# Products of constants that nobody reads, put on TensorE's queue in five places of a two-block transformer kernel

## The chip, the cores and the metric

The kernel runs on one core of one Trainium2 chip. The metric is the device time of one execution in microseconds. The names of the engines in the rows: PE is TensorE (matmul), PEld its weight load, DVE is VectorE, ACT is ScalarE, POOL is GpSimd, SP is SyncE.

## The reference: what is computed

Two blocks follow each other on a sequence of 512 tokens of width 1024 (8 tiles of 128 features), all in float32.

```
# first block: condition, normalise, project, two mixers, project out
mod = silu(c) @ w_ada + b_ada;  shift, scale, gate = split(mod, 3)
h = rms_norm(x, norm_g) * (1 + scale) + shift
ssm_u, ssm_z, q, k, v, attn_z, q_idx, k_idx, w_idx = split(h @ w_in)
y = concat(s5_mixer(ssm_u) * silu(ssm_z), dsa_mixer(q, k, v, q_idx, k_idx, w_idx) * silu(attn_z)) @ w_out
x = x + gate * y
# second block
h = rmsnorm(x, norm_mix_pre);  proj = h @ w_in2
merged = sum over 3 branches (retention, gla, swa) of sigmoid(gates) * (branch @ w_branch)
x = x + rmsnorm(merged @ w_out2, norm_mix_post)
h = rmsnorm(x, norm_ffn_pre)
x = x + rmsnorm((silu(h @ w_gate) * (h @ w_up)) @ w_down, norm_ffn_post)
```

## The kernel before

Each engine has one instruction stream, written out by hand, and semaphores between them. Features lie on partitions, the 512 tokens along the free dimension. A weight tile `w_raw` of 1024 x 256 numbers is streamed in by SyncE (three slots), ScalarE casts it to fp32r (`w_hi`, L1092), and VectorE writes the rest (`w_lo`, L1623). Activations are split likewise into `h_hi` and `h_lo` (or `y_`, `f_`), so that each product of a GEMM is three fp32r matmuls: hi by hi, lo by hi, hi by lo. A `gemm` has two halves, each into one of the PSUM banks 0 to 2; a half of kind "fm" is 8 input tiles by 3 matmuls of 128x512, one of kind "tm" is 2 x 8 x 3 matmuls of 128x256. All of these are recorded at L499, the helper `mm`.

Between stages stands a normalisation. ScalarE squares each of the 8 tiles into `sqb` (two buffers), TensorE sums the squares over the partitions by a product with the constant `ones` (`stats`, `last_stats`), in plain float32, ScalarE takes the root (L1112), and VectorE the reciprocal `rstd` (L1643). Then VectorE and ScalarE make the 8 tiles of `h_hi` and `h_lo` one after another (L1654, L1100, L1638), and TensorE waits for each: in `gemm_half`, with `need` given, matmuls of input tile k wait for `act_low` of k. For the two norms of the second block's end ("post1", "norm2"), VectorE also updates `xr` tile by tile (L1587, L2284) between them, and each square of "norm2" waits for its `xr` tile.

The five places of the change, by name:

- Place 1: after `modulation(3)`, ahead of the GEMM "k_idx". `modulation` turns a row by products of a single row and a single column (`ones` by `mrow`). k_idx waits for its weight tile (`w_low`) and for the input tiles of "norm0", which are made by L1800, L1143 and L1786.
- Place 2: after the first value GEMM, ahead of the four products `sgb` by `rstd` (8 rows high, 512 columns), which spread the norms of the keys (`kr_psum`) and wait for VectorE's reciprocal at L1921. The second value GEMM follows.
- Place 3: after `last_stats("norm1")`, ahead of the GEMM "swa_k" with `need=AT["norm1"]`.
- Place 4: after `last_stats("post1")`, ahead of `stats("norm2")`.
- Place 5: after `stats("norm2")`, ahead of the GEMMs "ffn_up" with `need=AT["norm2"]`.

`cst` and `ones` are float32 tensors in SBUF (`ident` is a part of `cst`); banks 3 to 7 serve statistics and attention.

Of the kernel before, what the change touches and what calls it, by code (L numbers as in the profile page):

```python
# [20 lines left out]
SEQ = 512  # L21
# [135 lines left out]
def hybrid_blocks(nc, wstream, xT, vecs, consts, head_rows, onehot, rel_bias, ssm_vec, ssm_b, ssm_c, d_skip,  # L157
                  alpha2, decay, reset, outT):
    f32, f32r, i32 = mybir.dt.float32, mybir.dt.float32r, mybir.dt.int32
    ALU, ACT, AX = mybir.AluOpType, mybir.ActivationFunctionType, mybir.AxisListType  # L160
    G, STREAM = plan()
    SPLIT_TILES = sum(kind == "split" for kind, _, _ in STREAM)
    SPLIT_AT = [i for i, (kind, _, _) in enumerate(STREAM) if kind == "split"]

# [6 lines left out]
    with ctx:  # L171
        def sb(name, shape, dt=f32):
            return ctx.enter_context(nc.sbuf_tensor(name, shape, dt))
# [17 lines left out]
        cst = sb("cst", [P, 800])  # L191
# [6 lines left out]
        ones = sb("ones", [P, P])  # L198
# [79 lines left out]
        bank = [ctx.enter_context(nc.psum_tensor(f"bank{i}", [P, SEQ], f32)) for i in range(8)]  # L278
# [61 lines left out]
        def pbanks(gr):  # L340
            return 2 * gr.g % GEMM_BANKS, (2 * gr.g + 1) % GEMM_BANKS

        def uses(gr, half):

            return (2 * gr.g + half) // GEMM_BANKS

        def w_low_of(sl):

            return w_lo[:, SPLIT_AT[sl] % RAW_SLOTS, :, :]
# [26 lines left out]
        def stat_bank(name):  # L376

            return bank[STAT_BANK.get(name[:3], 4)]
# [118 lines left out]
        def _(pe):  # L497
            def mm(out, lhsT, rhs, start, stop):
                return pe.matmul(out, lhsT, rhs, start=start, stop=stop)  # L499

            def gemm_half(gr, half, kind, hi, lo, k0=0, permuted=False, need=None, count=1):

                kt, s = gr.kts[0], gr.s
                bk = pbanks(gr)[half]
                if uses(gr, half):
                    pe.wait_ge(bank_free[bk], uses(gr, half))
                pe.wait_ge(w_low, s + 1)
                wh, wl = w_hi[:, s % 2], w_low_of(s)
                if kind == "fm":
                    c = slice(half * P, half * P + P)  # L510
                    out = bank[bk][:, :]
                    for k in range(kt):
                        a = k0 + k
                        if need is not None and half == 0:
                            pe.wait_ge(act_low, need + k + 1)
                        mm(out, wh[:, k, c], hi[:, a, :], k == 0, False)
                        mm(out, wh[:, k, c], lo[:, a, :], False, False)
                        ins = mm(out, wl[:, k, c], hi[:, a, :], False, k == kt - 1)
                else:
                    for t in (2 * half, 2 * half + 1):  # L520
                        out = bank[bk][:, (t % 2) * WC:(t % 2) * WC + WC]
                        for k in range(kt):
                            a = k0 + k
                            if need is not None and t == 0:
                                pe.wait_ge(act_low, need + k + 1)
                            if permuted:

                                ah, al = (x[:, a, t:SEQ:4] for x in (hi, lo))
                            else:
                                ah, al = (x[:, a, t * P:t * P + P] for x in (hi, lo))  # L530
                            mm(out, ah, wh[:, k, :], k == 0, False)
                            mm(out, ah, wl[:, k, :], False, False)
                            ins = mm(out, al, wh[:, k, :], False, k == kt - 1)
                ins.then_inc(group_done, count)
# [18 lines left out]
            def gemm(gr, kind, hi, lo, k0=0, permuted=False, need=None, between=None):  # L553

                gemm_half(gr, 0, kind, hi, lo, k0, permuted, need)
                if between is not None:
                    between()
                gemm_half(gr, 1, kind, hi, lo, k0, permuted, need)

            def gemm_long(gr, hi, lo, need):  # L560

                b = pbanks(gr)
                for half in range(2):
                    pe.wait_ge(bank_free[b[half]], uses(gr, half))
                n_tiles, k_all, k_at = len(gr.kts), sum(gr.kts), 0
                for j, kt in enumerate(gr.kts):
                    s = gr.s + j
                    pe.wait_ge(w_low, s + 1)
                    wh, wl = w_hi[:, s % 2], w_low_of(s)
                    for half in range(2):  # L570
                        c = slice(half * P, half * P + P)
                        out = bank[b[half]][:, :]
                        for k in range(kt):
                            a = k_at + k
                            if half == 0:
                                pe.wait_ge(act_low, need + a + 1)
                            mm(out, wh[:, k, c], hi[:, a, :], a == 0, False)
                            mm(out, wh[:, k, c], lo[:, a, :], False, False)
                            ins = mm(out, wl[:, k, c], hi[:, a, :], False, a == k_all - 1)
                        if j == n_tiles - 1:  # L580
                            ins.then_inc(group_done, 1)
                        elif half == 1:
                            ins.then_inc(w_used, 1)
                    k_at += kt
# [14 lines left out]
            def turned(out, row):  # L599

                for m in range(4):
                    ins = mm(out[:, m:m + 1], row[0:1, m * P:m * P + P], ones[0:1, 0:1], True, True)
                ins.then_inc(ada_done, 1)

            def modulation(i):

                pe.wait_ge(mod_row, i + 1)
                turned(bank[4 + i], mrow[:, i * SEQ:(i + 1) * SEQ])

            def stats(name, lhsT):  # L610

                stats_of(name, lhsT, 0, sizes[name])

            def stats_of(name, lhsT, m0, m1):
                n, s0, r = sizes[name], SQ0[name], ROOT[name]
                if r and m0 == 0:
                    pe.wait_ge(root_ready, r)
                for m in range(m0, m1):
                    pe.wait_ge(sq_ready, s0 + m + 1)
                    mm(stat_bank(name)[:, :], lhsT, sqb[:, (s0 + m) % 2, :], m == 0, m == n - 1)\  # L620
                        .then_inc(sq_used, 1)


            def presummed(name):

                pe.wait_ge(root_ready, ROOT[name])
                pe.wait_ge(presum_ready, PRESUM.index(name) + 1)
                mm(stat_bank(name)[:, :], ones[:, :], rstd[:, :], True, False)

            def last_stats(name):  # L630

                for m in (6, 7):
                    pe.wait_ge(sq_ready, SQ0[name] + m + 1)
                    mm(stat_bank(name)[:, :], ones[:, :], sqb[:, m % 2, :], False, m == 7).then_inc(sq_used, 1)
# [8 lines left out]
            for i in range(8):  # L643
# [5 lines left out]
                if i % 2 and i > 1:  # L649
                    modulation(i // 2 - 1)  # L650
            modulation(3)

            gr = G["k_idx"][0]
            b = pbanks(gr)
# [64 lines left out]
            for w, gr in enumerate(G["q"]):  # L719
                for half in range(2):  # L720
                    n = 2 * w + half
# [20 lines left out]
            def output_strip(q):  # L742

                if q:
                    pe.wait_ge(strip_act, 2 * q)
                for i in range(4):
                    j = 4 * q + i
                    for r in range(2):
                        rows = slice(64 * r, 64 * r + 64)
                        out = bank[5 + r][0:GCH, i * P:i * P + P]  # L750
                        mm(out, bb_re[rows, j, :], cl_re[rows, j, 0:P], True, False)
                        ins = mm(out, bb_im[rows, j, :], cl_im[rows, j, 0:P], False, True)
                ins.then_inc(strip_psum, 1)
# [12 lines left out]
            key_stats(3)  # L766
            output_strip(3)
            gemm_half(G["v"][0], 1, "tm", h_hi, h_lo)
            pe.wait_ge(rstd_ready, ROOT["k"] + 1)
            pe.wait_ge(heads_loaded, 16)  # L770
            pe.wait_ge(strip_act, 8)
# [85 lines left out]
            for w, gr in enumerate(G["out1"]):  # L857
                gemm(gr, "fm", y_hi, y_lo, between=(lambda: presummed("norm1")) if w == 3 else None)
            last_stats("norm1")


            gemm(G["swa_k"][0], "fm", h_hi, h_lo, need=AT["norm1"])
# [197 lines left out]
            for w, gr in enumerate(G["out2"]):  # L1060
                gemm(gr, "fm", h_hi, h_lo, need=AT["merged"],
                     between=(lambda: presummed("post1")) if w == 3 else None)
            last_stats("post1")
            stats("norm2", ones[:, :])
            for gr in G["ffn_up"]:
                gemm(gr, "fm", h_hi, h_lo, need=AT["norm2"])
            for w, gr in enumerate(G["ffn_down"]):
# [1336 lines left out]
```

## Time and profile before

| | |
|---|---|
| Median of three runs | 1721.64 us (1721.3 to 1724.29) |
| Profiled execution, its own time | 1725.39 us |
| Its span | 1723.6 us |
| PE busy | 1608.2 us, 93% |
| DVE busy | 851.6 us, 49% |
| ACT busy | 590.3 us, 34% |
| Mean granted clock of TensorE | 0.96 |

The span is what the trace covers; 1.8 us of the profiled execution lie around it. The clock is given as a share of full speed: 1.00 stands for 2.4 GHz, 0.50 for 1.2 GHz, and a figure between them is a mean over a stretch that has both.

### The profile page before, as it was taken

What the parts mean: (1) busy time and instruction counts of PE and PEld (TensorE: products, weight loads), DVE (VectorE), ACT (ScalarE), POOL (GpSimd) and SP (SyncE); (2) the same over time, 40 slices, a digit from 0 to 9 for tenths busy, and PEclk for the clock granted to TensorE, in tenths of its full rate; (3) what the DMA queues carried; (4) which work ended last, traced back from release to release, by engine and by line L of the source; (5) the groups of instructions that cost most, each with busy time, mean ns of one, the idle gap of its engine ahead of it and who ended that gap; (6) DMA issues with size and microseconds to landing.
All of it is one profiled execution on the core that took longest, in us unless ns stands there. A gap on an engine that the chain in (4) does not pass through costs nothing.

```text
span 1723.6 us, 19376 instructions
## 1 busy us (share of the span) xinstructions
PE 1608.2 (93%) x7890; PEld 1246.0 (72%) x7890; DVE 851.6 (49%) x1359; ACT 590.3 (34%) x861; POOL 23.1 (1%) x34
## 2 busy tenths in 40 slices
PE   6899989888789999999999999999997899999995
PEld 2476775655568778877778987888874688888884
DVE  3787887445444366524452544553335533333233
ACT  2334313344323355613342643243233322223220
POOL 0002010000000000000000000000000000000000
PEclk9898989888899999999999999999999999999998
DMA  8323143200332221211222222122231122222221
GB/s 290 139 76 97 51 82 141 74 25 1 123 139 82 73 74 49 75 51 72 73 90 101 87 74 74 69 79 98 98 124 72 53 96 98 97 98 92 97 105 49
DMA packets 23272, 152.26 MB, mean 88 GB/s; under 512 B 3328, under 2 KB 3888, under 8 KB 6912
## 3 DMA queue, kind: packets, MB, share of 16 engines
q1 hardware_dynamic: 20720, 137.43, 22.4%
q0 software_dynamic: 2464, 13.59, 2.8%
q8 instruction: 63, 1.03, 0.2%
q14 instruction: 25, 0.20, 0.0%
HBM read 144.55 MB, written 7.88 MB: 88 GB/s over the span
## 4 chain that ended last, share of the span: by engine, by line
PE 87%; DVE 8%; ACT 2%; issue 1%; DMA 1%; SPq 0%; ACTq 0%; DVEq 0%
PE bank L499 85%; DVE w_lo L1623 1%; PE bank L828 1%; DVE rstd L1643 1%; PE bank L891 1%; ACT w_hi L1092 1%; DVE sgb L1587 1%; DMA w_raw<-wstream 1%; DVE tval L1654 1%; DVE h_lo L1638 1%; DVE tval L1580 1%; DVE score L1840 0%; DVE xr L2284 0%; DVE down L2319 0%; DVE small L1839 0%
## 5 line engine op out<-in xcount | busy, mean ns | idle before, releaser
L499 PE MATMUL bank<-h_hi,w_hi 128*128 128x512 f32 x1160 | 471.6, 407 | 26.1 <-DVE h_lo L1638 17.9
L499 PE MATMUL bank<-h_hi,w_lo 128*128 128x512 f32 x1160 | 460.4, 397 | 0.0
L499 PE MATMUL bank<-h_lo,w_hi 128*128 128x512 f32 x1160 | 460.2, 397 | 0.0
L1623 DVE TENSOR_TENSOR w_lo<-w_raw,w_hi 128x2048 fp32r<-128x2048 f32 (+2 forms) x114 | 256.9, 2254 | 324.9 <-ACT w_hi L1092 323.4
L499 PEld LDWEIGHTS bank<-h_hi,w_hi 128*128 128x128 f32 x1160 | 222.4, 192 | 85.7 <-issue 24.6
L1092 ACT CAST w_hi<-w_raw 128x2048 fp32r<-128x2048 f32 (+2 forms) x114 | 213.7, 1876 | 187.2 <-PE bank L499 182.3
L499 PEld LDWEIGHTS bank<-h_hi,w_lo 128*128 128x128 f32 x1160 | 221.9, 191 | 48.8
L499 PEld LDWEIGHTS bank<-h_lo,w_hi 128*128 128x128 f32 x1160 | 222.8, 192 | 45.9 <-issue 1.4
L499 PE MATMUL bank<-y_hi,w_hi 128*128 128x512 f32 x272 | 111.8, 411 | 3.4 <-issue 3.4
L499 PE MATMUL bank<-y_hi,w_lo 128*128 128x512 f32 x272 | 106.5, 392 | 0.0
L499 PE MATMUL bank<-y_lo,w_hi 128*128 128x512 f32 x272 | 106.4, 391 | 0.0
L499 PE MATMUL bank<-w_hi,h_hi 128*128 128x256 f32 x352 | 102.9, 292 | 0.0
L499 PE MATMUL bank<-w_lo,h_hi 128*128 128x256 f32 x352 | 101.1, 287 | 0.0
L499 PE MATMUL bank<-w_hi,h_lo 128*128 128x256 f32 x352 | 100.9, 287 | 0.0
L1352 ACT ACTIVATE sgb<-bank 128x512 f32<-128x512 f32 x40 | 23.9, 598 | 166.6 <-PE bank L499 166.6
L499 PEld LDWEIGHTS bank<-w_hi,h_hi 128*128 128x128 f32 x352 | 69.0, 196 | 8.1 <-issue 8.0
L499 PEld LDWEIGHTS bank<-w_lo,h_hi 128*128 128x128 f32 x352 | 69.1, 196 | 0.0
L499 PEld LDWEIGHTS bank<-w_hi,h_lo 128*128 128x128 f32 x352 | 69.1, 196 | 0.0
L499 PE MATMUL bank<-f_hi,w_hi 128*128 128x512 f32 x176 | 68.5, 389 | 0.0
L499 PE MATMUL bank<-f_hi,w_lo 128*128 128x512 f32 x176 | 68.5, 389 | 0.0
L499 PE MATMUL bank<-f_lo,w_hi 128*128 128x512 f32 x176 | 68.5, 389 | 0.0
L499 PEld LDWEIGHTS bank<-y_hi,w_hi 128*128 128x128 f32 x272 | 51.5, 189 | 16.6 <-issue 6.0
(328 smaller groups left out, 1807.4 us busy)
## 6 DMA issues: line engine op xcount, KB each, us to landing
w_raw<-wstream SPq DMA_DIRECT2D x120, 1024.0 KB, 4.8
xr<-xT SPq DMA_DIRECT2D x2, 2048.0 KB, 8.3
w_raw<-wstream SPq DMA_DIRECT2D x4, 768.0 KB, 4.2
bias_rows<-bias_table POOLq DMA_DIRECT2D x1, 2560.0 KB, 15.2
bias<-bias_rows POOLq DMA_DIRECT2D x1, 2048.0 KB, 8.7
x_saved<-xr POOLq DMA_DIRECT2D x1, 2048.0 KB, 9.6
xr<-x_saved POOLq DMA_DIRECT2D x1, 2048.0 KB, 8.3
outT<-down SPq DMA_DIRECT2D x8, 256.0 KB, 2.0
```

Of the source, the lines that this page charges most:

```text
L499: return pe.matmul(out, lhsT, rhs, start=start, stop=stop)
L828: ins = pe.transpose(bank[PT_BANKS[i % 2]][:, s * P:s * P + P], prob(i, qt)[:, s * P:s * P + P], ident)
L891: ins = pe.transpose(bank[ST_BANKS[t % 2]][:, j * P:j * P + P], lg[:, n % 2, j, kb * P:kb * P + P], ident)
L1092: act.copy(w_hi[:, s % 2, 0:kt, :], w_raw[:, i % RAW_SLOTS, 0:kt, :]).then_inc(w_high, 1)
L1352: act.activation(sgb[:, m % 2, :], bank[bk][:, :], func).then_inc(bank_free[bk], 1)
L1580: settle(dve.tensor_tensor(out, a, b, op))
L1587: settle(dve.scalar_tensor_tensor(out=out, in0=a, scalar=s, in1=b, op0=op0, op1=op1))
L1623: dve.tensor_tensor(w_low_of(s)[:, 0:kt, :], w_raw[:, i % RAW_SLOTS, 0:kt, :], w_hi[:, s % 2, 0:kt, :].bitcast(f32), ALU.subtract).then_in ...
L1638: dve.tensor_tensor(dst, tval[:, a % 2, :] if src is None else src, hi.bitcast(f32), ALU.subtract).then_inc(act_low, 1)
L1643: dve.reciprocal(rstd[:, :], root[:, :]).then_inc(rstd_ready, 1)
L1654: dve.scalar_tensor_tensor(out=t, in0=src[:, m, :], scalar=gain(m), in1=rstd[:, :], op0=ALU.mult, op1=ALU.mult).then_inc(act_val, 1)
```

## The change

A new function `busy(b, n)` issues n matmuls with `ones` as the stationary and the first 512 columns of `cst` as the moving operand, into bank b. They wait for no semaphore and raise none. It is called in the five places: 14 into bank 3, 8 into bank 7, 15 into bank 4, and twice 11 into bank 5, 59 in all. Nothing reads what they write.

```diff
+            def busy(b, n):
+
+                for _ in range(n):
+                    mm(bank[b][:, :], ones[:, :], cst[:, 0:SEQ], True, True)
...
             modulation(3)
+            busy(3, 14)
...
             gemm_half(G["v"][0], 1, "tm", h_hi, h_lo)
+            busy(7, 8)
             pe.wait_ge(rstd_ready, ROOT["k"] + 1)
...
             last_stats("norm1")
+            busy(4, 15)
...
             last_stats("post1")
+            busy(5, 11)
             stats("norm2", ones[:, :])
+            busy(5, 11)
             for gr in G["ffn_up"]:
```

On TensorE at place 1, from the end of the last `modulation` to the first input tiles of k_idx, the changed kernel has these rows (`cst` and `ones` are the constants, `h_hi`, `h_lo` the input, `w_hi`, `w_lo` the weights of k_idx):

```order
L499 MATMUL bank<-ones,mrow 128x1 [waits mod_row]
L499 MATMUL bank<-ones,mrow 128x1 x3
L499 MATMUL bank<-cst,ones 128x512 x14
L499 MATMUL bank<-h_hi,w_hi 128x512 [waits act_low,w_low]
L499 MATMUL bank<-h_lo,w_hi 128x512
L499 MATMUL bank<-h_hi,w_lo 128x512
L499 MATMUL bank<-h_hi,w_hi 128x512 [waits act_low]
```

The 14 products stand ahead of the wait for `w_low` and `act_low`, and all else is as it was.

On TensorE at place 2 the difference is one row, between the last matmul of the first value GEMM and the products that wait for `rstd`:

```order
 L499 MATMUL bank<-w_lo,h_hi 128x256
 L499 MATMUL bank<-w_hi,h_lo 128x256
+L499 MATMUL bank<-cst,ones 128x512 x8
 L499 MATMUL bank<-rstd,sgb 128x512 [waits strip_act,heads_loaded,rstd_ready]
 L499 MATMUL bank<-rstd,sgb 128x512 x3
```

The four products by `rstd` come behind the eight.

On TensorE at places 4 and 5, around the sums of squares of "norm2", the changed kernel has:

```order
L499 MATMUL bank<-sqb,ones 128x512 [waits sq_ready] x2
L499 MATMUL bank<-cst,ones 128x512 x11
L499 MATMUL bank<-sqb,ones 128x512 [waits sq_ready,root_ready]
L499 MATMUL bank<-sqb,ones 128x512 [waits sq_ready] x7
L499 MATMUL bank<-cst,ones 128x512 x11
L499 MATMUL bank<-h_hi,w_hi 128x512 [waits act_low,w_low,bank_free1]
```

Eleven products stand on either side of the eight sums of "norm2"; place 3 looks like the second of these, with 15 products. No other engine's stream is changed.

## Rows read from the trace of the kernel before

**Rows 1.** The page: chain that ended last, share of the span by engine.

```profile
PE 87%; DVE 8%; ACT 2%; issue 1%; DMA 1%; SPq 0%; ACTq 0%; DVEq 0%
```

**Rows 2.** Timeline, PE, place 1: start us, us, what, [idle before <-releaser].

```profile
56.59 1.94 PE L499 MATMUL bank<-ones,mrow 1*128 1x1 f32 x16
66.10 0.79 PE L499 MATMUL bank<-h_hi,w_hi 128*128 128x512 f32 x1 [7.58 <-DVE w_lo L1623]
...
69.53 0.39 PE L499 MATMUL bank<-h_hi,w_lo 128*128 128x512 f32 x1
...
78.63 0.39 PE L499 MATMUL bank<-h_hi,w_hi 128*128 128x512 f32 x1
```

**Rows 3.** Busy time and granted clock (the 1.00 or 0.50 near the end), places 1 to 3.

```profile
59.00:59.50 0.50, 0.00 (x0) 0.00 (x0) 0.50 (x1) 0.00 (x0) 0.00 (x0) 0.61 1.16 492
...
236.50:237.00 0.50, 0.50 (x2) 0.29 (x1) 0.47 (x2) 0.00 (x0) 0.50 (x2) 0.60 0.13 16
238.00:242.00 4.00, 4.00 (x6) 1.33 (x4) 2.44 (x4) 0.00 (x0) 0.00 (x0) 0.50 0.91 94
...
246.50:247.00 0.50, 0.50 (x5) 0.50 (x5) 0.47 (x3) 0.00 (x0) 0.00 (x0) 0.66 1.05 101
...
517.20:523.00 5.80, 5.76 (x13) 3.62 (x14) 5.66 (x9) 2.47 (x4) 0.00 (x0) 0.50 0.08 35
```

**Rows 4.** Timeline, PE, a float32 pair of products with ones, back to back.

```profile
759.75 1.88 PE L499 MATMUL bank<-on,ones 128*128 128x512 f32 x4
```

**Rows 5.** Instructions that read the tile on: duration ns min/median/max.

```profile
L499 PE MATMUL bank<-on,ones x16: 591/592/593, 759.7 to 859.3; 128*128 128x512 f32 x16
```

**Rows 6.** Timeline, PE, place 2.

```profile
231.50 0.28 PE L499 MATMUL bank<-w_hi,h_lo 128*128 128x256 f32 x1
236.13 6.76 PE L499 MATMUL bank<-rstd,sgb 8*128 8x512 f32 x8 [4.35 <-DVE rstd L1921]
...
256.07 0.28 PE L499 MATMUL bank<-w_hi,h_lo 128*128 128x256 f32 x1
```

**Rows 7.** Busy time and granted clock after a short stall.

```profile
136.00:138.00 2.00, 0.70 (x2) 0.29 (x2) 2.00 (x2) 0.05 (x1) 1.62 (x2) 0.90 0.72 116
...
142.00:144.00 2.00, 2.00 (x6) 1.52 (x6) 1.69 (x10) 0.00 (x0) 0.50 (x1) 0.50 0.50 74
144.00:146.00 2.00, 2.00 (x10) 1.62 (x9) 1.73 (x9) 0.00 (x0) 0.00 (x0) 0.89 0.89 373
```

**Rows 8.** Timeline, PE, place 3.

```profile
509.64 1.13 PE L499 MATMUL bank<-sqb,ones 128*128 128x512 f32 x2 [0.65 <-ACT sqb L1106]
...
517.24 0.77 PE L499 MATMUL bank<-h_hi,w_hi 128*128 128x512 f32 x1 [6.47 <-DVE h_lo L1638]
...
527.05 0.40 PE L499 MATMUL bank<-h_hi,w_hi 128*128 128x512 f32 x1
```

**Rows 9.** Timeline, PE, places 4 and 5.

```profile
1313.74 1.97 PE L499 MATMUL bank<-sqb,ones 128*128 128x512 f32 x4
1322.15 6.59 PE L499 MATMUL bank<-sqb,ones 128*128 128x512 f32 x10 [6.43 <-ACT sqb L1106]
...
1330.49 1.13 PE L499 MATMUL bank<-sqb,ones 128*128 128x512 f32 x2 [0.37 <-ACT sqb L1106]
1331.99 1.13 PE L499 MATMUL bank<-sqb,ones 128*128 128x512 f32 x2 [0.37 <-ACT sqb L1106]
1339.67 0.76 PE L499 MATMUL bank<-h_hi,w_hi 128*128 128x512 f32 x1 [6.55 <-DVE h_lo L1638]
...
1345.13 0.50 PE L499 MATMUL bank<-h_hi,w_hi 128*128 128x512 f32 x1 [0.43 <-DVE h_lo L1638]
```

**Rows 10.** The chain that ended last, in order of time.

```profile
66.10 23.57 PE bank L499 x96
...
189.28 2.29 DVE w_lo L1623
...
525.48 62.28 PE bank L499 x318
```

## The prediction

> **What bounds the kernel now.** The chain that ended last comes first: 87% of it is TensorE and 8% VectorE [rows 1]. So time that TensorE loses in a stretch where it is the chain is paid in full, and so is time that it wins. Next the timeline of TensorE at the five places, for the length of each idle stretch and for who ends it. Place 1: 7.58 us, ended by VectorE's `w_lo` [rows 2]. Place 2: 4.35 us, ended by the reciprocal [rows 6]. Place 3: 6.47 us, ended by the first `h_lo` [rows 8]. Places 4 and 5: 6.43 us, ended by the first square, and 6.55 us, ended by `h_lo` [rows 9]. Then the granted clock around them: after such a stretch it stands at 0.50, the lower of the two levels, and TensorE begins its next work there [rows 3]. At place 1 the first eight matmuls of k_idx take 3.43 us, from 66.10 to 69.53, where the later ones start 0.228 us apart (40 from 69.53 to 78.63) [rows 2]: 1.6 us lost. At place 2 the clock falls between 236.5 and 237 and rises between 246.5 and 247 [rows 3]. These stretches are what the added products can change, so two questions decide: does a product fit the gap, and what sets the pace behind it.
>
> **What one product costs.** It is a plain float32 product, 128x128 by 128x512. The nearest row is the pair of products with `ones` at 759.75: four records for two products, so each product is two records, in 1.88 us from first start to last end [rows 4]. One record lasts 0.592 us [rows 5], so starts lie (1.88 - 0.592) / 3 = 0.43 us apart and a product costs 0.86 us at the higher level. At the lower level the four products by `rstd` show it: 6.76 us for eight records [rows 6], which is about 1.7 us each. Hence 14 products are 12.0 us, 8 are 6.9, 15 are 12.9 and 11 are 9.5 at the higher level. All five are longer than their gaps. The products don't wait for anything and end late by a fixed amount; the question is who has been waiting.
>
> **Place 1.** `modulation(3)` ends at 58.5 (56.59 + 1.94) [rows 2]. The products end at 58.5 + 12.0 = 70.5, where k_idx started at 66.10. From there its 48 matmuls start 0.228 us apart: 70.5 + 10.9 = 81.4, against 78.63 for the next GEMM now [rows 2]. That is 2.8 us later: 4.4 of overrun less 1.6 regained. All of its input is there by then, since the kernel before runs at that pace from 69.53 on, so nothing else is saved. The chain is TensorE from 66.10 on for 23.57 us and then reaches the VectorE stretch by way of a weight split whose cast waits for TensorE's use of a tile [rows 10], so I take 2.8 as paid in full.
>
> **Place 2.** The first value GEMM ends at 231.6, eight products end at 238.5, and then come the four by `rstd`, ready since 236.1. At the higher level they take 3.4 and the second value GEMM, 96 matmuls 0.12 us apart, 11.5: its end comes at 253.4. Now the last one starts at 256.07 [rows 6], so it ends its turn at 256.2: 2.8 us earlier. But the clock will hardly stay up. In the trace before it was low over the whole of 238 to 242, while those products of only eight rows kept TensorE busy, and rose 3.9 us after the GEMM behind them began [rows 3]. A fall after a stall of only 2.6 us at 136 shows also how such a dip looks: 0.50 until about 144.4, more than 6 us [rows 7]. I put a dip of 3.4 us, about the length of the four products, against the gain; at half speed that is 1.7 us. Place 2 gives 2.8 - 1.7 = 1.1 us. Bounds: 2.8 with no dip, 0 with one of 6 us.
>
> **Place 3.** The last sum of squares starts at 509.64 and takes its 0.86 [rows 8]; fifteen products end at 510.5 + 12.9 = 523.4. Between 517.24 and 527.05 TensorE did 24 matmuls in which each three waited for an `h_lo` of VectorE. The clock was low there until 523 [rows 3], but low or high made no difference to the end, since three matmuls take 1.3 us even at the lower level and VectorE delivers a tile in 1.4 (the steps of the like stretch at place 5: four from 1339.67 to 1345.13) [rows 9]. The first half could start as late as 527.05 - 24 x 0.228 = 521.6 and still end in time. It starts at 523.4, 1.8 us too late, and from 525.48 on TensorE is the chain for 62 us [rows 10]. Cost: 1.8 us.
>
> The Trainium skill (TensorE: Matmul & The Clock Gate, Terms) prices time at the lower clock by its length times the missing share, which is half. By it place 3 would get back 2.9 us for its 5.8 us at 0.50 [rows 3], and the 15 products would be nearly worth their place. The trace speaks against it there: matmuls that wait for VectorE don't come earlier at a faster clock.
>
> **Places 4 and 5.** At place 4 eleven products end at 1315.5 + 9.5 = 1325.0, 2.9 us after the first square was ready (1322.15) [rows 9]. The eight sums then need 0.86 us each, and now they settle at one per 1.50 us, which is the pace of VectorE's `xr` tiles (1330.49 to 1331.99) [rows 9]. Even with the squares' two buffers in turn the backlog is gone by the seventh sum (1325.0 + 6 x 0.9 = 1330.4, against 1330.49). The last sum stays at 1331.99: cost 0, with 0.1 us to spare; if it runs over, some tenths. At place 5 the products end at 1332.85 + 9.5 = 1342.3, against a start of 1339.67. Three matmuls in 0.69 us catch up with one `h_lo` per 1.4 by the fifth tile, 1342.3 + 4 x 0.69 = 1345.1, which now starts at 1345.13 [rows 9]. Cost 0, and no gain, though the clock is kept up at both.
>
> **The sum.** 2.8 - 1.1 + 1.8 + 0 + 0 = +3.5 us. The profiled execution would go from 1725.39 to 1728.9. It lies 3.75 above the median of the runs, 1721.64, to which the same sum gives 1725.1. A dip at place 1 can add to it: the single-row products of `modulation` didn't hold the clock (it falls between 59.0 and 59.5, 0.5 us after them) [rows 3], and if it still falls there, about 3.4 us at half speed cost another 1.7. With these bounds the forecast's own range is +1.8 (no dip at all) to +6.3 (3.5 + 1.1 + 1.7), so 1723.4 to 1727.9. Chance 0.60.
>
> **The rivals.**
>
> *The delay of place 1 is absorbed.* From 189.28 VectorE is the chain for most of 47 us, until the reciprocal at 236 [rows 10]. If VectorE has work of its own there that a late TensorE doesn't delay, the 2.8 us vanish: -1.1 + 1.8 = +0.7, or -1.0 with no dip at place 2, so 1720.6 to 1722.3. Against it: that stretch opens with a weight split released from TensorE. Chance 0.13.
>
> *Half of the low clock's time comes back and every overrun counts.* If TensorE and not VectorE sets the pace at places 3 to 5, place 3 costs 6.2 - 2.9 = 3.3 instead of 1.8, place 4 costs 2.9 less about 2.3 (five sums in 6.59 us [rows 9] instead of 4.3), place 5 2.6 less 1.4 (six matmuls at 0.43 instead of 0.23). That adds 1.5 + 0.6 + 1.2 = 3.3: 1728.4. The rule of TensorE: Matmul & The Clock Gate in the Trainium skill would have it so. Against it stand the VectorE releasers of [rows 9]. Chance 0.09.
>
> *Faster: a product of constants is only one record long.* If the same stationary were loaded once and the product cost 0.43 us, place 1 would end at 64.5, ahead of 66.10, and win 1.6; place 2 would end at 235.0 and win 256.2 - (236.1 + 3.4 + 11.5) = 5.2, or 3.5 with the dip; place 3 would cost nothing. That is -5.1 to -6.8, so about 1715.8. It decides below 7.6 / 14 = 0.54 us a product. Against it: `ones` is the same stationary in the pair of [rows 4] too, and it has four records. Chance 0.08.
>
> *Constants don't hold the clock,* as rows of height 1 and 8 didn't. Then most of the 59 products cost 1.7 us: places 1 and 3 alone would run over by some 15 and 14 us, and the time is above 1755. Against it: at place 4 the clock came up while only sums with `ones` ran (1.13 us for the two records of a sum from 1330.49 on is the higher level) [rows 9]. Chance 0.04. Some 0.06 are left for what I haven't seen, such as stalls elsewhere that fall on another moment of the clock.
>
> **How the numbers follow.** A measurement of this kernel tells 0.2%, 3.4 us, from no change: faster is below 1718.2, slower above 1725.1. The forecast lies on that upper bound, so half of its 0.60 is slower (0.30), with 0.09 and 0.04 of the rivals and 0.02 of the rest: 0.45. Faster has 0.08 and 0.02: 0.10. The rest, 0.45, is the same. The range from 1719.8 to 1729.5 takes in the forecast, the absorbed delay and the paced rival, and leaves out 0.16.
>
> **What would show it.** In the trace after: 28 records at place 1, 0.43 us apart, the first `h_hi` matmul at 70.5 with no VectorE wait ahead of it, and the GEMM behind k_idx at 81.4; at place 2 the end of the second value GEMM about 1.1 us closer to the end of the first, with a stretch at 0.50 around it; at place 3 the second half of swa_k 1.8 us further from the last sum; at places 4 and 5 unchanged distances between the last square of "post1", the last sum of "norm2" and the second half of the first ffn_up GEMM, with the clock at 1.00 throughout. The prediction is wrong if the products show one record each, if they run at 0.85 us a record, or if the distance from k_idx to the reciprocal at L1921 hasn't grown.

## The result, and the profile after

The changed kernel took 1729.4 us in the median of six runs (1725.71 to 1732.02), the kernel before beside it 1721.46 (1719.69 to 1724.29). The ratio is 1.0045 with a 95% interval of 1.0028 to 1.0061, so the change made the kernel slower by 4.8 to 10.5 us. Timed twice more beside other kernels it gave 1.0034 (1.0023 to 1.0046) and 1.0035 (1.0022 to 1.0047): about +6 us. The forecast was +3.5 us, with bounds of its own from +1.8 to +6.3. The sign and the two later times fit it; the first time, +7.9, lies above these bounds.

The page of the changed kernel, as [rows 1], with the line of busy time ahead:

```profile
PE 1643.1 (95%) x8008; PEld 1262.5 (73%) x8008; DVE 852.0 (49%) x1359; ACT 590.5 (34%) x861; POOL 23.1 (1%) x34
...
PE 91%; DVE 5%; ACT 2%; issue 1%; DMA 1%; SPq 0%; DVEq 0%; ACTq 0%
```

TensorE has 118 more records, which is 59 products of two records each, and 35 us more of busy time, and it is 91% of the chain instead of 87%. VectorE and ScalarE do what they did.

Place 1 on TensorE, against [rows 2]:

```profile
56.91 1.94 PE L499 MATMUL bank<-ones,mrow 1*128 1x1 f32 x16
58.78 12.28 PE L499 MATMUL bank<-cst,ones 128*128 128x512 f32 x28
70.50 0.79 PE L499 MATMUL bank<-h_hi,w_hi 128*128 128x512 f32 x1
...
81.83 0.39 PE L499 MATMUL bank<-h_hi,w_hi 128*128 128x512 f32 x1
```

The 28 records take 12.28 us, which with the 0.59 us of a last record is 0.43 us from one start to the next. No wait stands ahead of 70.50: VectorE had written `w_lo`, for which TensorE waited before, at 66.4. From the start of `modulation`'s last products to the GEMM behind k_idx it is 24.9 us (56.91 to 81.83), against 22.0 before (56.59 to 78.63): +2.9.

Place 2, against [rows 6]:

```profile
234.84 7.03 PE L499 MATMUL bank<-cst,ones 128*128 128x512 f32 x16
241.80 3.69 PE L499 MATMUL bank<-rstd,sgb 8*128 8x512 f32 x8
...
258.39 0.28 PE L499 MATMUL bank<-w_hi,h_lo 128*128 128x256 f32 x1
```

The four products by `rstd` last 3.69 us instead of 6.76, at the higher clock. From the last matmul of the first value GEMM (0.12 us ahead of the first row) to the last of the second it is 23.7 us, against 24.6 before: -0.9. The busy time and granted clock of the same stretches, against [rows 3]:

```profile
59.00:70.00 11.00, 11.00 (x26) 4.82 (x26) 8.75 (x14) 5.04 (x6) 0.00 (x0) 1.00 0.19 80
...
241.80:245.50 3.70, 3.70 (x10) 1.48 (x9) 2.24 (x3) 0.00 (x0) 0.00 (x0) 1.00 0.92 94
246.50:250.00 3.50, 3.50 (x20) 3.50 (x19) 3.33 (x9) 0.00 (x0) 0.00 (x0) 0.52 0.92 80
251.00:255.00 4.00, 4.00 (x35) 4.00 (x35) 3.79 (x10) 0.59 (x1) 0.00 (x0) 1.00 0.02 4
```

The clock stays at 1.00 through place 1. At place 2 it holds during the products of eight rows and then falls for 3.5 us under the dense GEMM behind them: 20 matmuls ran in that time, where some 30 would fit at 0.12 us each.

Place 3, against [rows 8]:

```profile
511.49 1.12 PE L499 MATMUL bank<-sqb,ones 128*128 128x512 f32 x2 [0.65 <-ACT sqb L1116]
512.45 13.04 PE L499 MATMUL bank<-cst,ones 128*128 128x512 f32 x30
524.92 0.79 PE L499 MATMUL bank<-h_hi,w_hi 128*128 128x512 f32 x1
```

The 24 matmuls of the first half now run without a wait, 0.23 us apart, and the second half starts at 530.8. That is 19.3 us after the last sum, against 17.4 before (509.64 to 527.05): +1.9. Places 4 and 5, against [rows 9]:

```profile
1316.03 1.97 PE L499 MATMUL bank<-sqb,ones 128*128 128x512 f32 x4
1317.84 9.61 PE L499 MATMUL bank<-cst,ones 128*128 128x512 f32 x22
1327.28 6.74 PE L499 MATMUL bank<-sqb,ones 128*128 128x512 f32 x14
1334.28 1.12 PE L499 MATMUL bank<-sqb,ones 128*128 128x512 f32 x2 [0.27 <-ACT sqb L1116]
1335.25 9.60 PE L499 MATMUL bank<-cst,ones 128*128 128x512 f32 x22
1348.82 0.50 PE L499 MATMUL bank<-h_hi,w_hi 128*128 128x512 f32 x1 [0.43 <-DVE h_lo L1648]
```

Seven of the eight sums run in a row (6.74 us), and the eighth again waits for a square. From the sums of "post1" to that last sum it is 18.25 us, before and after (1313.74 to 1331.99). The matmuls behind catch up with VectorE at 1348.82, which is 14.5 us after the last sum and one tile later than forecast. Both places cost nothing.

### The profile page after: what moved, and what is told of

Its sections match the earlier page's. It is cut to its first block, busy times and chain, and to the rows that moved or that the text cites. A ratio compares the mean times of both kernels' runs of the same rounds, so it can differ in the third digit from the quotient of the medians.

```text
span 1725.9 us, 19612 instructions
## 1 busy us (share of the span) xinstructions
PE 1643.1 (95%) x8008; PEld 1262.5 (73%) x8008; DVE 852.0 (49%) x1359; ACT 590.5 (34%) x861; POOL 23.1 (1%) x34
## 4 chain that ended last, share of the span: by engine, by line
PE 91%; DVE 5%; ACT 2%; issue 1%; DMA 1%; SPq 0%; DVEq 0%; ACTq 0%
PE bank L499 89%; PE bank L835 1%; PE bank L899 1%; DMA w_raw<-wstream 1%; DVE sgb L1597 1%; DVE w_lo L1633 1%; DVE rstd L1653 1%; ACT w_hi L1102 0%; DVE xr L2294 0%; DVE down L2329 0%; DVE tval L1664 0%; DVE h_lo L1648 0%; DVE score L1879 0%; DVE sqb L1992 0%; ACT sgb L1209 0%
```

## The experiments

All were timed against the kernel before on the same chip. Microseconds are worked out as the ratio less 1, times 1721.5. The four kernels with one place each were timed on a chip where the kernel before had a median of 1723.62 us; it had 1721.28 and 1721.58 on the chips of the later runs.

**One place at a time.** Each kernel keeps the calls of `busy` in one place (two for 4 and 5) and drops the others, as here for place 1:

```diff
             modulation(3)
             busy(3, 14)
...
-            busy(7, 8)
...
-            busy(4, 15)
...
-            busy(5, 11)
```

> Only the 14 products ahead of k_idx are kept. The theory of the prediction (a product costs 0.86 us, the overrun of 4.4 us less 1.6 us of regained low clock is paid in full) expects +2.8 us on the kernel before, up to +4.5 with a fall of the clock at the place. The rival that the delay is absorbed by VectorE's stretch expects 0. The rival that the measured total of +7.9 us instead of +3.5 comes from stalls of the attention stage (about 311 to 470 us) that meet the clock at another moment expects more than +4 here, with more low clock in that stretch.

Measured: 1.0018 (1.0009 to 1.0027), +3.1 us (1.5 to 4.6). The overrun is paid; the absorbed delay is out. Its one trace doesn't bear out the rival of the attention stage either: that stage was 145.90 us, against 149.07 before (table below).

> Only the 8 products ahead of the four by rstd are kept. The theory of the prediction expects -1.1 us (2.8 us earlier, less a dip of 3.4 us at half speed). Bounds: -2.8 without the dip, 0 with one of 6 us. The rival of the attention stage expects a time off these bounds, with a distance from here to the end of that stage that has grown.

Measured: 0.9989 (0.9979 to 0.9999), -1.9 us (-3.6 to -0.2), within the bounds. The trace has the forecast dip: the clock fell for 3.4 us, 1.2 us behind the products of eight rows.

> Only the 15 products ahead of swa_k are kept. The theory of the prediction expects +1.8 us, since 12.9 us of products leave too little room for 24 matmuls ahead of the last input tile. The rival that TensorE sets the pace there (its whole overrun less half of the low clock's time) expects +3.3.

Measured: 1.0018 (1.0009 to 1.0028), +3.1 us (1.5 to 4.8). This interval doesn't tell 1.8 from 3.3; the trace does, with the same +1.9 us as in the whole change (table below).

> Only the two groups of 11 products around the sums of norm2 are kept. The theory of the prediction expects 0 (VectorE's tiles set the pace, and the backlog of TensorE is gone in time). The rival that TensorE sets the pace expects +1.8 (0.6 at place 4, 1.2 at place 5).

Measured: 1.0001 (0.9992 to 1.0010), +0.2 us (-1.4 to +1.7). The interval ends just short of the +1.8 of the rival, and the traces settle it at 0 (74.77 us before, 74.79 with the products).

**The stages, apart.** A single time scatters by 2 us, so the stages were compared between the traces. The marks are starts of the same ScalarE instructions in every kernel; in the trace of before they stand at 14.2, 73.4, 200.6, 250.6, 320.9, 470.0, 527.2, 1275.0, 1327.7 and 1349.7 us. The last column is the sum of the two stages from 1275.0 to 1349.7.

```
kernel               start  place 1        place 2          attention  place 3          place 4+5
                     14.2   73.4   200.6   250.6   320.9    470.0      527.2   1275.0   1349.7
before               14.20  59.19  127.23  50.01   70.28    149.07     57.27   747.71   74.77
only_place1          14.83  62.25  127.46  50.04   70.42    145.90     57.30   749.30   74.78
only_place2          13.41  59.49  127.30  49.11   70.65    148.27     57.30   744.78   74.80
only_place3          14.65  59.51  127.29  49.99   70.26    148.57     59.19   746.23   74.79
only_places4_5       13.27  60.33  127.50  50.85   70.57    145.99     57.29   747.69   74.79
after                14.85  61.74  127.25  49.11   70.65    148.23     59.18   746.24   74.78
all_five_again       13.03  62.75  127.72  47.62   72.19    142.87     59.18   746.11   74.78
all_five_third       14.14  61.44  127.20  49.12   70.61    148.23     59.17   748.97   74.78
places1_and_3        13.21  62.61  127.66  50.46   70.30    145.26     59.18   746.09   74.78
place3_with_11       13.36  59.25  127.29  50.75   70.52    145.40     57.29   744.61   74.77
place2_with_5        14.32  59.62  127.38  45.17   68.96    148.31     57.27   747.47   74.78
all_five_fitted      13.24  57.62  127.30  46.70   70.64    148.41     57.28   747.45   74.77
fitted_1_2_only      13.88  57.97  127.58  45.18   68.98    148.28     57.29   747.47   74.77
places4_5_with_16    14.01  60.07  127.53  50.78   70.53    145.44     57.28   744.66   78.55
```

The stages of the five places are sharp: place 3 is 57.3 us without its 15 products and 59.2 with them, in all 14 traces; place 1 is 59.2 to 60.3 without and 61.4 to 62.8 with (means 59.6 and 62.2, +2.5). The attention stage is not: 142.9 to 149.1, whatever the kernel; neither is the long stage from 527 on, 744.6 to 749.3, nor the start. Two stretches of 149.1 us, from 320.9 us on, of the changed kernel in its first and its second profile:

```profile
320.90:470.00 149.10, 122.29 (x496) 79.63 (x495) 72.30 (x203) 62.96 (x129) 0.56 (x1) 0.84 0.13 50
```

```profile
320.90:470.00 149.10, 122.29 (x519) 80.06 (x518) 73.06 (x204) 63.69 (x130) 0.56 (x1) 0.89 0.14 50
```

The same program has a mean clock of 0.84 in the one and of 0.89 in the other, and does more matmuls in the same time in the second. Taken between its own marks, the attention stage has 47.8 us at the lower clock in the first and 34.1 in the second, and is 5.4 us shorter there. Where TensorE stops for a moment again and again, whether the clock falls at a stop differs from one execution to the next.

**The whole change again.**

> The changed kernel itself, timed again beside the others. The four runs with one part each gave the ratios 1.0018, 0.9989, 1.0018 and 1.0001, together +4.5 us. The theory that the parts add up and that the first measurement of +7.9 us lay high by chance expects +3 to +6 us. The rival that the parts cost more together than apart (a stall that only all five cause, in the attention stage or elsewhere) expects +7 to +9 again.

Measured: 1.0034 (1.0023 to 1.0046), +5.8 us (4.0 to 7.9). The first +7.9 was on the high side; the parts' +4.5 lies inside. The profiled execution, 1721.93 us, is the fastest of its twelve (median 1727.42), so its trace is not a typical one.

**A count at place 3 that ends in time.** `busy(4, 15)` becomes `busy(4, 11)`, and the other places are empty.

> Place 3 alone, with 11 products instead of 15. They end at about 520.0, ahead of the 521.6 from which the 24 matmuls still end in time. The theory that the cost of place 3 is the late start alone expects 0, where 15 products cost +3.1 us (1.5 to 4.8). The rival that TensorE sets the pace from 517.24 on expects 520.0 - 517.2 = 2.8 less half of the low clock's time that is regained (up to 2.9): 0 to +2.8, with the sum of squares and the second half of swa_k further apart than before.

Measured: 1.0002 (0.9988 to 1.0015), +0.3 us (-2.1 to +2.6).

```profile
507.19 9.61 PE L499 MATMUL bank<-cst,ones 128*128 128x512 f32 x22
516.23 0.80 PE L499 MATMUL bank<-h_hi,w_hi 128*128 128x512 f32 x1
...
520.68 0.49 PE L499 MATMUL bank<-h_hi,w_hi 128*128 128x512 f32 x1 [0.42 <-DVE h_lo L1644]
```

The matmuls start 2.5 us after VectorE has the first tile (513.7) and are waiting for it again at 520.68. The stage is 57.29 us, as without any product: only a start later than VectorE's lead allows costs anything.

**A count at place 2 that ends in time.** `busy(7, 8)` becomes `busy(7, 5)`, alone.

> Place 2 alone, with 5 products instead of 8: they end at 235.9, ahead of the reciprocal at 236.1. The theory (no overrun, and the clock is up when the products by rstd start, with a dip of 3.4 us afterwards) expects -3.4 us, against -1.9 with 8 products. The rival that the products of eight rows bring the clock down for as long as before expects 0 to -1.

Measured: 0.9986 (0.9977 to 0.9995), -2.4 us (-4.0 to -0.9).

```profile
232.33 4.45 PE L499 MATMUL bank<-cst,ones 128*128 128x512 f32 x10
```

```profile
236.80:240.50 3.70, 3.67 (x9) 1.45 (x9) 3.53 (x10) 0.00 (x0) 1.84 (x3) 1.00 0.88 108
240.50:246.00 5.50, 5.50 (x47) 5.50 (x47) 5.26 (x12) 0.00 (x0) 0.00 (x0) 1.00 1.00 95
```

In this execution the clock didn't fall around the place, and the stage was 4.8 us shorter than before (45.17 against 50.01). With the same count in the next experiment it fell from 238.7 on, and the stage was 46.70. The stage and the next one, from 200.6 to 320.9, are 114.1 us together here, 6.7 less than the mean of 120.8 in the seven traces without products at place 2. Yet the whole is only 2.4 us faster, and this execution is a typical one (1718.99 us, the median being 1718.77). So part of what place 2 gives is lost elsewhere; the attention stage is 148.3 us here, against 145.3 to 146.0 in five of those seven.

**All places with counts that end in time.**

```diff
-            busy(3, 14)
+            busy(3, 8)
...
-            busy(7, 8)
+            busy(7, 5)
...
-            busy(4, 15)
+            busy(4, 7)
...
-            busy(5, 11)
+            busy(5, 7)
```

> All five places, with counts that end ahead of what ends the gap at 0.86 us a product: 8, 5, 7, 7 and 7 instead of 14, 8, 15, 11 and 11. Theory: place 1 gains its 1.6 us of low clock, place 2 gains 5.1 us, or 3.4 with a dip of 3.4 us behind the products of eight rows, the other three give nothing: -5.0 to -6.7 us. The rival that the clock falls anyway, since now TensorE idles up to 2 us behind the products at places 1, 3, 4 and 5 expects about -3.4 (place 2 alone).

Measured: 0.9969 (0.9958 to 0.9980), -5.3 us (-7.2 to -3.4). Place 1 on TensorE:

```profile
57.42 7.13 PE L499 MATMUL bank<-cst,ones 128*128 128x512 f32 x16
65.07 0.50 PE L499 MATMUL bank<-h_hi,w_hi 128*128 128x512 f32 x1 [0.52 <-DVE w_lo L1633]
```

Eight products end 0.5 us ahead of `w_lo`, and k_idx starts at once with 0.23 us a matmul. The stage is 57.62 us, 2.0 less than the mean without products, where 14 products make it 2.5 longer. The two stages from 200.6 to 320.9 are 117.3 us, 3.5 less; together that is -5.5, close to the -5.3 measured. The rival is out: the clock stayed up although TensorE idled behind the products, as here at place 3:

```profile
511.00:525.00 14.00, 11.37 (x42) 7.39 (x43) 11.13 (x15) 6.09 (x8) 0.00 (x0) 1.00 0.04 18
```

> The fitted counts at places 1 and 2 (8 and 5), and nothing at places 3 to 5. The theory that places 3 to 5 are paced by VectorE at either clock expects the same as all five fitted, about -5.3 us. The rival that the kept-up clock is worth something there too expects less, -3 us or so.

Measured: 0.9950 (0.9937 to 0.9964), -8.6 us (-10.8 to -6.2), so products at places 3 to 5 aren't needed. This is faster than the forecast of -5.3, and than all five fitted; but the stages of places 3 to 5 are equal in both traces (57.28 and 57.29, 74.77 and 74.77), although the clock is 1.00 throughout these stages in the one and falls at all three places in the other. The 2 us between the two spans come from the two stages around place 2, whose code is the same: 3.2 us less there, and some 1 us more ahead of them. It was the fastest kernel that was run, median 1712.23 us beside 1721.58. The stages of its one trace give 1.7 us less at place 1 and 6.7 less in the two around place 2, together -8.4. But it was timed in five runs only, and the profiled one (1717.09) is the slowest of them.

**Too many at places 4 and 5.** Both calls `busy(5, 16)`, alone.

> Places 4 and 5 alone, with 16 products each instead of 11. The theory (hidden only as long as the backlog is gone before the last tile) expects that now both cost: at place 4 the products end at about 1329.3 and the last of eight sums starts at 1335.3 instead of 1332.0, +3.3; at place 5 they end 13.8 us after the last sum and 24 matmuls follow, 13.8 + 5.5 = 19.3 us instead of the 16.6 between the last sum and the second half, +2.7. Together +6.0 us. The rival that these places are hidden whatever the count expects 0.

Measured: 1.0037 (1.0025 to 1.0050), +6.4 us (4.3 to 8.6).

```profile
1310.91 13.90 PE L499 MATMUL bank<-cst,ones 128*128 128x512 f32 x32
1324.64 7.60 PE L499 MATMUL bank<-sqb,ones 128*128 128x512 f32 x16
1332.08 13.90 PE L499 MATMUL bank<-cst,ones 128*128 128x512 f32 x32
1345.41 0.80 PE L499 MATMUL bank<-h_hi,w_hi 128*128 128x512 f32 x1
```

All eight sums are now behind their squares, and the GEMM runs without a wait. The stages grew by 3.8 us up to the mark at 1349.7 and by 2.7 behind it (376.50 from there to the end, against 373.8 in all the others).

**Two places together, and the whole a third time.**

> The two places that run over at a cost, 14 and 15 products, without the other three. The theory that parts add up expects the +2.7 and +1.9 us that the stages show apart, so +4.6 us (or +6 by the medians of the two runs, 3.1 and 3.1). The rival that the whole change costs more together than apart (+5.8 and +7.9 us were measured, +4.5 is the sum of the parts) expects +7 or more already here, since place 2 gives 2 back.

Measured: 1.0023 (1.0014 to 1.0033), +4.0 us (2.4 to 5.7). The two overruns add up.

> The changed kernel a third time, beside the run of places 1 and 3 on the same chip. The theory of added parts expects that it is about 2 us faster than places 1 and 3 alone, so +3 to +5 us on the kernel before. The rival of an unexplained extra cost expects +6 or more.

Measured: 1.0035 (1.0022 to 1.0047), +6.0 us (3.8 to 8.1). It was expected to be 2 us faster than places 1 and 3 alone and was 2 us slower. The intervals hardly leave room for the expectation: less 1.9 us, the interval of places 1 and 3 is +0.5 to +3.8, and the one measured here begins at +3.8. So the whole seems to cost more than its parts; the next section says where to look.

## Why the prediction was right or wrong

*The price of a product* was right: 0.86 us for two records, from a pair at 759.75, against 28 records in 12.28 us. The rivals of one record, and of constants that don't hold the clock, are out: 1.00 from 59 to 70.

*Place 1*: +2.8 us forecast, +2.9 in the first trace and +2.5 in the mean of the stages, +3.1 when timed alone. It is paid in full; the stage behind it, from 73.4 to 200.6, is 127.2 to 127.7 with and without the products. The dip that might have added 1.7 us came in none of the five traces with 14 products: the clock was 1.00 over the whole stage in all of them.

*Place 2*: -1.1 us forecast with a dip of 3.4 us. The stage was 0.9 shorter with such a dip in two traces of the whole change and in the one of place 2 alone (49.11 or 49.12 against 50.01). In the second trace of the whole change the clock did not fall there:

```profile
246.00:250.00 4.00, 4.00 (x36) 4.00 (x35) 3.79 (x10) 0.00 (x0) 0.00 (x0) 1.00 0.98 87
```

That stage was 2.4 shorter, but the next one was 1.9 longer, with the clock at 0.50 from 277.6 to 284.4. The two stages together are 119.8 us in all four traces with eight products and 120.8 in the mean of the seven without: -1.1, as forecast. Timed alone it gave -1.9. The mechanism was right; that the dip had the length of 3.4 us was a guess in the prediction, and here it came out.

*Place 3*: +1.8 forecast, +1.9 in every trace. Right, and 11 products cost nothing, as the latest start of 521.6 said. *Places 4 and 5*: 0 forecast and 0.0 measured; 16 products cost +6.4 where the same working gave +6.0. So the margin was real, and the rule of half the low clock's time is refuted at places 3 to 5: with 7 to 11 products the clock was up and nothing came of it. The Trainium skill's price (TensorE: Matmul & The Clock Gate, Terms) holds at place 1, where TensorE alone sets the pace: eight products won 2.0 us in the stage in one trace and 1.7 in the other, and the low clock had cost 1.6 by [rows 2].

*The sum* is where the prediction falls short. It gave +3.5, and three measurements gave +7.9, +5.8 and +6.0, with intervals that all begin above 3.5 (at 4.8, 4.0 and 3.8). The terms by the stages of the traces, +2.5 - 1.1 + 1.9 + 0 = +3.3, are those of the forecast, so no term was mis-sized: what the sum lacks is 2.5 us or more outside the five places, which it put at nothing but for "stalls elsewhere that fall on another moment of the clock". The median of 1729.4 us lies 0.1 us below the top of the widest range stated, 1729.5, which was drawn so far up for the rival of TensorE's pace, and the runs refute that rival. That it lies inside is luck. The medians of the two later measurements, 1727.42 and 1726.31, lie in the mechanism's own range of 1723.4 to 1727.9, near its top.

*Where the rest is.* The record gives the mean granted clock of every run, and with two levels only, the time at the lower one is 2 x (1 - clock) x span. It is 127 us in the mean of the kernel before and 94 in the changed kernel (clocks 0.963 and 0.973), the same on two chips: 33 us less. In the traces the stages of the five places have 51 us at the lower clock without products and 10 with them: 41 us less. So outside these stages the changed kernel has some 8 us more at the lower clock than the kernel before. Over the runs of one and the same kernel, each us at the lower clock goes with 0.2 to 0.4 us of time, so 8 are worth 2 to 3 us, an estimate that about closes the sum. The same count for places 1 and 3 alone leaves nothing over (19 us less in the runs, and as much in the stages), and their +4.0 is what the stages say. For five products at place 2 alone it leaves some 10 (5 less in the runs, 16 in the stages), and there too the runs gave 4 us less than the stages. For eight at place 2 alone it leaves no surplus (13 less in the runs, 9 in the stages).

Why the clock is lower elsewhere, and in which stage, stays open. In six of the seven traces with products at place 2 the attention stage has 47.8 us at the lower clock and lasts 148.2 to 148.4 us; in five of the seven without it has 41.0 to 44.4 and lasts 145.3 to 146.0. That is a hint, not a proof: two without have 148.6 and 149.1, and the seventh with products has 142.9, in an execution that is the fastest of its twelve.

## What to carry to other kernels

Work that only keeps an engine's clock up must end before what ends the wait, and its own price decides. Here a product costs 0.86 us: in a gap of 7.6 us, 14 cost 2.5 us and eight won 1.7 to 2.0; in a gap of 4.4 us, eight won 1.9 when timed alone and five 2.4. It pays only where the engine itself sets the pace behind the wait; where another engine hands over tiles one by one, a faster clock buys nothing, and the added work is free only as long as the engine can still catch up before the last tile. Where a total scatters by more than the effect, compare the stages between fixed marks in the traces, and then check their sum against the total of many runs: here every stage came out as forecast and the total did not.

## What the runs showed of the hardware that was not expected

The products of eight rows held TensorE busy for 3.69 us at the full clock, and the fall came behind them, under dense work, from 246.6 to 250.0. In four of the seven traces with products at place 2 the clock fell 1.1 to 1.3 us behind them; in the other three, with the same rows, it did not fall there at all. So the clock of a stretch can't be read from what TensorE does in it alone, and it differs between executions of one program. The attention stage of the changed kernel differs by more than 5 us between two executions (142.9 and 148.2 us) with 34.1 and 47.8 us at the lower clock. Over 35 runs of the kernel before on one chip the mean clock goes from 0.959 to 0.966 and the time from 1726.7 to 1718.5 us, with a correlation of -0.8. So most of the scatter of this kernel's times on one core goes with TensorE's clock.
